# Mixer units of 256 columns: pooling and convolution inputs as hi and lo side by side, convolution from SBUF

## The reference

```python
proj = h @ w_in
...
rq, rk, rv, rg, pu, sz, sxbc, sdt, fq, fk, fv, ff, gl = jnp.split(proj, points, axis=-1)
...
y_b = pool_mixer(pu, pool_w, pool_scale)          # windows of 2, 4, 8, 16 over time, less pu
...
xbc = jax.nn.silu(causal_depthwise_conv(xbc, conv_w, conv_b))   # 4 taps over time
dt = jax.nn.softplus(dt_raw.astype(F32) + dt_bias.astype(F32))
```

## Time and profile before

| | |
|---|---|
| runs, median (lowest to highest) | 1485.44 us (1485.1 to 1485.89), 3 runs |
| profiled execution, its own time | 1485.3 us |
| its span | 1483.3 us |
| granted TensorE clock, mean | 0.999 |
| busy PE, DVE, ACT, POOL | 99%, 79%, 55%, 4% |
| chunks 5 to 23 of the mixer, layer 0 and layer 1 | 234 to 292 us, 959 to 1017 us |

### The profile page before, as it was taken

One profiled execution on the slowest core, in us unless ns is written; L12 is line 12 of the kernel. 1 busy time (PEld: TensorE's weight loads), 2 busy tenths in 40 slices (PEclk: granted clock), 3 DMA queues, 4 the chain that ended last, 5 costly groups with the idle time before them and its releaser, 6 DMA issues.

```text
span 1483.3 us, 20030 instructions
## 1 busy us (share of the span) xinstructions
PE 1471.6 (99%) x7735; PEld 1245.1 (84%) x7735; DVE 1170.6 (79%) x1430; ACT 820.6 (55%) x1032; POOL 56.8 (4%) x56
## 2 busy tenths in 40 slices
PE   8999999999999999999999999999999999999998
PEld 5788889987988888888888888898888888788886
DVE  6888777878799878879787897777879988775663
ACT  4545465566563466556465564654746545664543
POOL 0000003200000000000000000050000000000000
PEclk9999999999999999999999999999999999999999
DMA  9899976556777857888768887665567787566652
GB/s 347 294 320 305 332 229 199 169 170 186 224 250 243 285 161 242 261 276 282 244 227 262 274 280 251 192 186 158 180 196 242 247 260 250 171 186 185 196 188 99
DMA packets 211813, 342.91 MB, mean 231 GB/s; under 512 B 18547, under 2 KB 134515, under 8 KB 211718
## 3 DMA queue, kind: packets, MB, share of 16 engines
q1 hardware_dynamic: 193574, 275.56, 58.5%
q10 hardware_dynamic: 18144, 66.07, 13.3%
HBM read 340.53 MB, written 1.05 MB: 230 GB/s over the span
## 4 chain that ended last, share of the span: by engine, by line
PE 95%; DVE 2%; SPq 1%; ACT 1%; DMA 1%; issue 0%; DVEq 0%; ACTq 0%
PE ps L849 12%; PE ps L798 11%; PE ps L789 11%; PE ps L799 11%; PE ps L963 6%; PE ps L965 6%; PE ps L964 6%; PE ps L854 6%; PE ps L821 3%; PE ps L1313 3%; PE ps L897 3%; PE ps L1315 3%; PE ps L1314 3%; PE ps L819 2%; PE ps L1003 1%; DVE xbc L2115 1%
## 5 line engine op out<-in xcount | busy, mean ns | idle before, releaser
L1386 ACT ACTIVATE w_hi<-w_raw 128x1024 fp32r<-128x1024 f32 x490 | 505.0, 1051 | 247.5 <-DMA w_raw<-in_w_ffn_out 70.6
L1738 DVE TENSOR_TENSOR w_lo<-w_raw,w_hi 128x1024 fp32r<-128x1024 f32 x480 | 575.3, 1222 | 79.3 <-ACT w_hi L1386 79.1
L798 PE MATMUL ps<-w_hi,h_both 128*128 128x512 f32 x586 | 231.1, 394 | 0.0
L799 PE MATMUL ps<-w_lo,h_both 128*128 128x512 f32 x586 | 228.3, 390 | 0.0
L789 PE MATMUL ps<-w_hi,h_both 128*128 128x512 f32 x586 | 227.6, 390 | 0.0
L849 PE MATMUL ps<-h_both,w_hi 128*128 128x512 f32 x768 | 206.6, 394 | 0.0
L1754 DVE SCALAR_TENSOR_TENSOR ada_acc<-ada_slab,c_silu,ada_acc 128x1024 f32<-128x1024 f32 x128 | 163.8, 1279 | 6.1 <-DMA ada_slab<-in_w_ada 6.1
L849 PEld LDWEIGHTS ps<-h_both,w_hi 128*128 128x128 f32 x768 | 132.9, 189 | 19.2
L963 PE MATMUL ps<-w_hi,act_hi 128*128 128x512 f32 x352 | 137.6, 391 | 0.0
L965 PE MATMUL ps<-w_hi,act_lo 128*128 128x512 f32 x352 | 137.0, 389 | 0.0
L964 PE MATMUL ps<-w_lo,act_hi 128*128 128x512 f32 x352 | 137.0, 389 | 0.0
(11 more groups left out here) (318 smaller groups left out, 2100.0 us busy)
## 6 DMA issues: line engine op xcount, KB each, us to landing
w_raw<-in_w_ffn_in SPq DMA_DIRECT2D x352, 256.0 KB, 3.8
w_raw<-in_w_in SPq DMA_DIRECT2D x168, 512.0 KB, 3.8
ada_slab<-in_w_ada ACTq DMA_DIRECT2D x126, 512.0 KB, 4.7
w_raw<-in_w_ffn_out SPq DMA_DIRECT2D x88, 512.0 KB, 4.4
w_raw<-in_w_ssm_out SPq DMA_DIRECT2D x16, 512.0 KB, 4.6
w_raw<-in_w_out SPq DMA_DIRECT2D x16, 512.0 KB, 3.4
ada_slab_first<-in_w_ada SPq DMA_DIRECT2D x14, 512.0 KB, 7.2
w_raw<-in_w_pool_out SPq DMA_DIRECT2D x8, 512.0 KB, 3.8
```

Source lines behind the costliest of these rows:

```text
L798: mm(out, hi[:, k, tok(tt)], wh[:, cs], start=(k == 0), stop=False)
L799: mm(out, hi[:, k, tok(tt)], wl[:, cs], start=False, stop=False)
L1386: fn(WH[:, n % N_HI, 0:width], RAW[:, n % N_RAW, 0:width], ACT.Copy).then_inc(w_hi, 1)
L1738: dve.tensor_tensor(WL[:, n % N_RAW, 0:width], RAW[:, n % N_RAW, 0:width], WH[:, n % N_HI, 0:width], ALU.subtract).then_inc(w_lo, 1)
```

## The change

`pu` becomes two units of two chunks and `xbc` six, all in the form of `half_unit_chunk`. The sum of hi and lo now lies in SBUF: for pu in its own tile, for xbc in a new tile `conv_in`, two buffers of two tiles each, in space that x_dt takes later. Tap 0 (ACT) and the other taps (DVE) read `conv_in`, two tiles at a time, one chunk after the unit ended. A bank pair is freed by the lo add (`half_ok`), a `conv_in` buffer by the last tap. The dt transposes on PE move from chunk 7 to 6, the z step on DVE from 8 to 6, since the second pu half needs their banks.

```diff
-MIX = [("fv", C_FV, 4, True), ("dtff", 0, 1, True), ("pu", C_PU, 4, False)]
-MIX += [("xbc", C_XBC + HALF * j, 4, False) for j in range(3)]
+MIX = [("fv", C_FV, 4, True), ("dtff", 0, 1, True)]
+MIX += [("pu", C_PU + T * j, 2, False) for j in range(2)]
+MIX += [("xbc", C_XBC + T * j, 2, False) for j in range(6)]
...
-HALVES = [i for i, m in enumerate(MIX) if m[0] in ("fq", "fk", "sz")]
+HALVES = [i for i, m in enumerate(MIX) if m[0] in ("pu", "xbc", "fq", "fk", "sz")]
+XBC_ENDS = [MIX_AT[i] + m[2] for i, m in enumerate(MIX) if m[0] == "xbc"]
...
+        CONV = at("conv_in", [P, 2, 2, T], F32, xdt_off)
...
-                if c == 7:
+                if c == 6:
                     pe.wait_ge(zf_ok.sem, zf_ok.at(layer, 1))
...
-                        if j == 0 and i in HALVES and freed[pair][0] is conv_ok:
-                            _, count = freed[pair]
-                            pe.wait_ge(conv_ok.sem, conv_ok.at(layer, count - 1))
-
-                            def second_bank():
-                                pe.wait_ge(conv_ok.sem, conv_ok.at(layer, count))
-                        elif j == 0 and freed[pair] is not None:
+                        if j == 0 and freed[pair] is not None:
...
                         if i in HALVES:
                             done(g)
+                            if name == "xbc" and HALVES.index(i) >= 4:
+                                act.wait_ge(conv_ok.sem, conv_ok.at(layer, HALVES.index(i) - 3))
                             fn(half_unit(i), PS[:, 2 * pair:2 * pair + 2, 0:T], ACT.Copy).then_inc(half_hi.sem, 1)
...
+                    for n in range(6):
+                        if c == XBC_ENDS[n] + 1:
+                            act.wait_ge(half_ok.sem, half_ok.at(layer, 3 + n))
+                            for t in range(2):
+                                k = 2 * n + t
+                                ins = fn(XBC[:, k, :], CONV[:, n % 2, t, :], ACT.Identity, scale=vec(layer, V_CW + 36 + k),
+                                         bias=vec(layer, V_CB + k))
+                            ins.then_inc(tap0_ok.sem, 1)
...
+            def conv_taps(layer, n):
+
+                dve.wait_ge(tap0_ok.sem, tap0_ok.at(layer, n + 1))
+                last = {}
+                for back in (1, 2, 3):
+                    for t in range(2):
+                        k = 2 * n + t
+                        if back > 1:
+                            chain.need(last[t])
+                        ins = dve.scalar_tensor_tensor(XBC[:, k, back:T], CONV[:, n % 2, t, 0:T - back],
+                                                       vec(layer, V_CW + 12 * (3 - back) + k), XBC[:, k, back:T], ALU.mult,
+                                                       ALU.add)
+                        if back < 3:
+                            last[t] = chain.mark(ins)
+                ins.then_inc(conv_ok.sem, 1)
...
                     split_to(g + 4)
+                    for n in range(6):
+                        if c == XBC_ENDS[n] + 1:
+                            conv_taps(layer, n)
...
-                    if c == 8:
+                    if c == 6:
                         dve.wait_ge(zt_ps.sem, zt_ps.at(layer, 1))
...
-                pool.wait_ge(pu_ok.sem, pu_ok.at(layer, 1))
+                pool.wait_ge(half_ok.sem, half_ok.at(layer, 2))
```

More of the change, by code:

```diff
@@ L458, in half_unit @@
             n = HALVES.index(i)
-            tile, first = ((FQ, 0), (FQ, 2), (FK, 0), (FK, 2), (SZ, 0), (SZ, 2), (SZ, 4), (SZ, 6))[n]
+            if 2 <= n < 8:
+                return CONV[:, n % 2, :, :]
+            tile, first = ((PU, 0), (PU, 2), (FQ, 0), (FQ, 2), (FK, 0), (FK, 2), (SZ, 0), (SZ, 2), (SZ, 4), (SZ, 6))[
+                n if n < 2 else n - 6]
             return tile[:, first:first + 2, :]
@@ L534, in build @@
         half_ok = Signal(sem("half_unit_lo_added"), len(HALVES))
-        pu_ok = Signal(sem("pool_u_ready"), 1)
         pwin_ok = Signal(sem("pool_windows_ready"), 1)
@@ L806, in token_chunk, with half_unit_chunk @@
                 return ins
-            def half_unit_chunk(g, j, banks, second_bank):
+            def half_unit_chunk(g, j, banks):
                 wh, wl = weights(g)
@@ L815, in half_unit_chunk @@
                         for bank, cs in tiles:
-                            if second_bank is not None and kk == 0 and bank > banks and not lo:
-                                second_bank()
                             if lo:
@@ L1200, in mixer_core @@
                     pe.wait_ge(ydx_ok.sem, ydx_ok.at(layer, 4))
-                    pe.wait_ge(half_ok.sem, half_ok.at(layer, 4))
+                    pe.wait_ge(half_ok.sem, half_ok.at(layer, 12))
                     for h in range(HEADS):
@@ L1266, in mixer @@
                 freed = [None, None]
-                n_gate, n_mul, n_pool, n_xbc = 0, 0, 0, 0
+                n_gate, n_mul, n_pool = 0, 0, 0
                 for i, (name, col, n, by_token) in enumerate(MIX):
@@ L1285, in mixer @@
                             continue
-                        second_bank = None
-                        if j == 0 and i in HALVES and freed[pair][0] is conv_ok:
-                            _, count = freed[pair]
-                            pe.wait_ge(conv_ok.sem, conv_ok.at(layer, count - 1))
-                            def second_bank():
-                                pe.wait_ge(conv_ok.sem, conv_ok.at(layer, count))
-                        elif j == 0 and freed[pair] is not None:
+                        if j == 0 and freed[pair] is not None:
                             sig, count = freed[pair]
@@ L1304, in mixer @@
                         if i in HALVES:
-                            half_unit_chunk(g, j, 2 * pair, second_bank).then_inc(w_used, 1)
+                            half_unit_chunk(g, j, 2 * pair).then_inc(w_used, 1)
                             continue
@@ L1325, in mixer @@
                         freed[pair] = (gmul_ok, n_mul)
-                    elif name == "xbc":
-                        n_xbc += 1
-                        freed[pair] = (conv_ok, 2 * n_xbc)
                     elif i in HALVES:
@@ L1333, in mixer @@
                     elif name != "dtff":
-                        freed[pair] = ({"pu": pu_ok, "rv": rv_ok, "rg": rg_ok}[name], 1)
+                        freed[pair] = ({"rv": rv_ok, "rg": rg_ok}[name], 1)
                 def before(k):
@@ L1559, in mixer @@
                 layer = s // 3
-                n_gate, n_xbc = 0, 0
+                n_gate = 0
                 for c in range(N_MIX - TAIL):
@@ L1575, in mixer @@
                             fn(ZF[0:20, :], PS[0:20, 2, 0:T], ACT.Copy).then_inc(zf_ok.sem, 1)
-                        if name == "pu":
-                            done(g)
-                            fn(PU[:], tiles, ACT.Copy).then_inc(pu_ok.sem, 1)
                         if i in HALVES:
                             done(g)
+                            if name == "xbc" and HALVES.index(i) >= 4:
+                                act.wait_ge(conv_ok.sem, conv_ok.at(layer, HALVES.index(i) - 3))
                             fn(half_unit(i), PS[:, 2 * pair:2 * pair + 2, 0:T], ACT.Copy).then_inc(half_hi.sem, 1)
@@ L1587, in mixer @@
                             fn(RG[:], both, ACT.Silu).then_inc(rg_ok.sem, 1)
[L1588 to L1596, removed]
                         if name in ("rq", "rk"):
@@ L1616, in mixer @@
                             n_gate += 1
+                    for n in range(6):
[6 more added lines that the diff above has]
+                            ins.then_inc(tap0_ok.sem, 1)
                     for n in range(4):
                         if c == SZ_ENDS[n] + 1:
-                            act.wait_ge(half_ok.sem, half_ok.at(layer, 5 + n))
+                            act.wait_ge(half_ok.sem, half_ok.at(layer, 13 + n))
                             fn(SZ[:, 2 * n:2 * n + 2, :], SZ[:, 2 * n:2 * n + 2, :], ACT.Silu).then_inc(sz_ok.sem, 1)
@@ L2090, in mixer @@
                 places = ada_places(s)
-                n_xbc, n_branch = 0, 0
+                n_branch = 0
                 for c in range(N_MIX - TAIL):
@@ L2099, in mixer @@
                         tiles = quad(2 * pair)
-                        if name in ("xbc", "rq", "rk") or i in HALVES:
+                        if name in ("rq", "rk") or i in HALVES:
                             split_to(g + 4)
@@ L2105, in mixer @@
                                 .then_inc(half_ok.sem, 1)
[L2106 to L2121, removed]
                         if name in ("rq", "rk"):
```

## The result

The changed kernel takes **1495.64 us** (median of 4 runs, 1493.99 to 1496.39) against 1485.55 of the kernel before on the same chip (4 runs): ratio 1.0067, 95% interval 1.0054 to 1.0079. It is slower, 0.7%. The profiled execution took 1496.14 us, its span is 1494.1.

What follows compares the result with a forecast made beforehand. PE's rate was taken to bound the kernel. Stalls of 6.15 us a layer less 1.7 saved give 4.45, twice 8.9, on the profiled 1485.3: 1494.2 us, range 1486 to 1500.

Steps and rivals of the forecast that it cites:

- PE's saving: pu and xbc products on PE: 1.4 us from 16 faster chunks plus 0.3 from a dropped wait, 1.7 a layer.
- The first stall: Before chunk 13: PE waits 2.3 us for the first xbc lo add, behind the dt chain and one GpSimd split.
- The cycle: Vector engine from add to add: split, six taps blocked by GpSimd's split, add; 6.15 to 6.55 us against PE's 5.58.
- Stall before chunk 15: PE waits 0.55 to 0.95 us, taken as 0.75, as the vector engine's cycle outlasts PE's two chunks.
- Chunk 21: Before chunk 21: PE waits 2.0 to 2.4 us, taken as 2.2, for the fourth xbc add.
- Chunk 23: Before chunk 23: PE waits 0.7 to 1.1 us, taken as 0.9; pooling products, splits, taps and add outlast its chunks.
- 17 and 19: Before chunks 17 and 19: no stall; chunk 16 carries cumulative sums, and later GpSimd's split misses the taps.
- Rival 3: PE's clock falls behind the stalls: 2.8 us more after each of two long stalls a layer, 1505 us; chance 0.07.
- rival 1: No stall in the mixer, only PE's saving shows: 1481.9 us, faster by 0.23%; chance 0.08.
- Rival 2: Only the stall before chunk 13 comes, since the new taps are not blocked: 1486.5 us; chance 0.12.
- Rival 4: The dt chain escapes GpSimd's split but the other stalls stand: 1489.6 us; chance 0.13.

Runs made afterwards that it cites:

- e3: Changed kernel with the Exp and dt chain at chunk 7 and all w_lo splits on the vector engine instead of GpSimd: 1481.74 us.
- e8: Changed kernel with Exp and dt chain at chunk 7 and taps of the first five xbc halves reading PSUM bank 7: 1481.38 us.
- e1: Changed kernel with the Exp on ACT and the dt chain on DVE both at chunk 7 instead of 9 and 10: 1491.31 us.
- e2: Changed kernel with the w_lo splits of chunks 15, 17, 19, 21 and 23 on the vector engine instead of GpSimd: 1485.93 us.
- e4: Changed kernel with taps of the first five xbc halves reading PSUM bank 7 instead of conv_in, result not computed: 1489.93 us.
- e5: Changed kernel with ten filler matmuls into an unused bank on PE ahead of chunk 13: 1494.43 us.
- e6: Changed kernel with filler matmuls ahead of chunk 13 and taps of the first five halves reading PSUM bank 7: 1486.52 us.

## Why the prediction was right, and where not

The forecast was 1494.2 us, 1.4 below the median; the sign, the place and the mechanism were right. One rival's effect was under-rated and its price turned out to be absorbed; that the sum came out so close in spite of it was not foreseen and in so far is luck.

- **PE's saving, 1.7 us a layer:** 1.70 in e3 and in e8, where nothing else is in the way; in e3 1.33 of it over chunks 5 to 20 (forecast 1.4), 0.37 behind them (0.3). 2 x 1.70 = 3.4 of e3's 3.67 us gain.
- **The first stall, 2.3:** 2.44 and, in layer 1, about the same. With 1.77 us taken off the clock of the profile, the chain's last operation ended at 258.7 (forecast 258.4), GpSimd's split began at 254.9 (255.1), the add ended at 259.3 (259.1). One split on the chain, not none and not two. e1 takes the whole stall away, e2 the 2.1 us of the split. One term ahead of it was under-sized: GpSimd's sum of 762 elements, put at some 0.8 us on the chain, cost it 1.26, since the sum itself took 2.31 us beside the `w_lo` split and not 1.46. So 1.30 us of the chain were left behind GpSimd's split, not 0.9. The sum and the chain's first operation in the changed kernel:

```profile
251.18 2.31 POOL L2372 TENSOR_TENSOR scratch_t<-pool_w 128x762 f32<-128x762 f32 x1
```

```profile
252.10 1.43 DVE L2152 TENSOR_SCALAR s<-e 128x40 f32<-128x40 f32 x1
```

- **The cycle, 6.15 to 6.55 us:** 6.35. Its pieces: six free taps cost 2.37 from start to the next operation in e2, the upper end (not the 2.0 of the L2184 row); blocked, 4.51, so one split costs 2.14 instead of 2.4. GpSimd's split started 2.15 us behind the add (1.9). That the conflict is in the two SBUF inputs, as the Trainium skill has it in "SBUF — State Buffer", section "Who interferes with whom", is shown for the taps by e4 and e8: the same taps with one input in PSUM never took over 0.483 us. One reading of the earlier trace rows was wrong: the `w_lo` split that took 1.82 us began at 276.32 and did not end with GpSimd's, at 277.07, but at 278.14: it gave up the time to 277.07 and then took its own 1.1. The 2.4 us a split is GpSimd's own time there and did not rest on this.
- **Stall before chunk 15, 0.75:** none, because of the step that failed. PE came to chunk 15 at 268.34 us, 1.66 late, when the add of 266.72 was done for 0.95. In e5, with the clock kept full, the stall is 0.69. **Chunk 21, 2.2:** 1.22, for the same reason (1.94 in e5). **Chunk 23, 0.9:** 0.89. 17 and 19: none, as forecast. The waits for the lo add are 8.0 us in PE's list and not about 12: 3.3 are what the clock took over, and 1.0 is the 0.17 by which the list counts each of the six waits short.
- **Rival 3, the clock, 0.07:** this was the wrong step: the forecast put the clock's fall at nothing, and the rival put it at 2.8 us behind each of two stalls. It does fall behind the first stall in each layer (1.66 us lost in layer 0, 1.7 in layer 1), not behind the second (1.22 us), and it does not add up as the rival's price had it. Chunk 21 can't start before the vector engine's fourth add, so a slower PE only waits less; the forecast sum stood at 6.15 and the measured one is 6.36. e5 shows this, and e6 the other side: with the taps free, filling the pause is worth 1.5 us a layer.
- **Rivals 1, 2 and 4:** e3 and e8 are rival 1 made true (1481.7 and 1481.4, forecast 1481.9). Rival 2, the first stall alone, was forecast at 1486.5: it is e4, 1489.93, or 1486.52 once the filler has taken the clock's part out (e6). Rival 4, the chain free, 1489.6: it is e1, 1491.31, the clock's fall at chunk 21 again in it.

e1's expectation failed in one step: the late pool windows were to bring a stall of 1.6 us before chunk 15, and they did not. Two of GpSimd's splits fell on the taps behind the second add instead and held chunk 17 by 0.45 us, and 21 was held by 2.38. Why the whole median is 1.4 above the forecast is not settled to that size: 2 x 0.2 us are losses inside the stretch, the remaining 1.0 is smaller than the spread that was seen ahead of the mixer (1.5 us between starts of the stretch), but no run isolates it.

## What to carry to other kernels

Moving a vector operand from PSUM to SBUF is no neutral edit when GpSimd works beside it: look up where every such operation will stand when GpSimd's next instruction starts, and whose hand-over stands behind it. When a new hand-over to the bounding engine is put into another engine's strict order, count what stands ahead of it, small dependent operations above all. And measure a side effect (here the clock) where nothing else binds: beside a second bound it cost nothing, without it 1.5 us a layer.

## What the runs showed of the hardware that was not expected

After a pause of 2.44 us of PE the granted clock was 0.62 over the next 4.45 us; after 2.38 us (e1) it was 0.65 over chunk 21, as this window shows:

```profile
283.74:288.01 4.27, 4.27 (x16) 3.70 (x17) 4.27 (x10) 4.27 (x6) 0.00 (x0) 0.65 0.21 75
```

In layer 1 the same pause was followed by a granted clock of 0.67 over 5.17 us. After 1.94 us (e5, ahead of chunk 21) and 1.48 (e2) the granted clock was 1.00 and the chunks took 2.89 and 2.91. The Trainium skill says in "TensorE: Matmul & The Clock Gate", Part 1, that the throttled state is the default and activity releases it; the rows agree in so far as a pause brought the lower level and work the full one back (1.00 from 267 to 275 us in the changed kernel).

The size of the vector operation did not matter: one of 40 elements took 2.27 us and ended with the GpSimd split of 1024 elements (2.45 us) that it had started beside. Nor did only operations with two tensor inputs stand still: the chain's first, with one, took 1.43 us beside GpSimd's sum, and 0.17 in the earlier trace rows. And it went the other way too, as the sum of 2.31 us above shows.
